# Norm behind the feed-forward part from three sums, half of the modulation moved, and a convolution that opens with two blocks

## The reference, cut to what matters

```python
# end of the first block
h = rmsnorm(x, g_ff_pre)
y = square(relu(h @ w_ff1)) @ w_ff2            # 1024 -> 4096 -> 1024
x = x + rmsnorm(y, g_ff_post)
# start of the second block, layer 0; a second layer (i = 1) follows with the mixer hgrn2
mod = silu(c) @ ada_w[i] + ada_b[i]            # 1024 x 6144 for each of 2 layers
sh1, sc1, g1, sh2, sc2, g2 = split(mod, 6)
h = rms_norm(x, norm1_g[i]) * (1 + sc1) + sh1
a, gate = split(h @ conv_w_in, 2)              # 1024 -> 2 x 1024
u = a * sigmoid(gate)
y = depthwise_conv(u, width 31) + dw_b         # 31 taps for each feature
y = silu(layer_norm(y)) @ conv_w_out
x = x + g1 * y
h = rms_norm(x, norm2_g[i]) * (1 + sc2) + sh2
x = x + g2 * (square(relu(h @ mlp_w1[i])) @ mlp_w2[i])
```

## Time and profile before

| | us |
|---|---|
| median of 3 runs | 2105.71 (2105.07 to 2106.84) |
| profiled execution, own time | 2106.69 |
| its span | 2104.9 |
| TensorE matmul busy | 2058.6 (98%) |
| VectorE busy | 1243.4 (59%) |
| ScalarE busy | 833.4 (40%) |
| POOL busy | 210.9 (10%) |
| mean granted TensorE clock | 0.995 |

### The profile page before, as it was taken

The page is one execution under the profiler, slowest core; times in us unless marked ns, Lnnn a source line. Parts: engine busy times, 40 slices in busy tenths (PEclk is TensorE's granted clock), DMA queues, the critical chain, the costliest instruction groups (busy, mean ns, idle before and its releaser), DMA issues.

```text
span 2104.9 us, 27545 instructions
## 1 busy us (share of the span) xinstructions
PE 2058.6 (98%) x11206; PEld 1668.5 (79%) x11206; DVE 1243.4 (59%) x1951; ACT 833.4 (40%) x1362; POOL 210.9 (10%) x182
## 2 busy tenths in 40 slices
PE   8999999999999999999999999999999989999998
PEld 7787987678878886666988888888887779888887
DVE  5566746446677777986644344476776756343443
ACT  5345544445323233225523233355464544232232
POOL 1321011010000004552000000100000010000002
PEclk9999999999999999999999999999999999999999
DMA  6313422026677762662233332221221232323331
GB/s 203 113 58 100 152 93 88 21 62 219 222 278 256 261 233 92 180 163 84 94 122 100 99 99 83 73 72 51 61 81 51 81 98 83 114 89 97 100 101 40
DMA packets 219710, 245.56 MB, mean 117 GB/s; under 512 B 9272, under 2 KB 205368, under 8 KB 213440
## 3 DMA queue, kind: packets, MB, share of 16 engines
q1 hardware_dynamic: 209360, 231.20, 33.9%
q10 hardware_dynamic: 10224, 12.61, 2.4%
HBM read 237.75 MB, written 3.78 MB: 115 GB/s over the span
## 4 chain that ended last, share of the span: by engine, by line
PE 86%; DVE 6%; ACT 4%; DMA 3%; issue 1%; POOL 0%; ACTq 0%; SPq 0%; DVEq 0%; POOLq 0%
PE bank L1439 24%; PE bank L1443 23%; PE bank L1447 23%; PE bank L1465 2%; PE bank L1473 2%; PE bank L1469 2%; DMA raw<-in_hgrn_in 1%; DVE wL L2067 1%; PE bank L1625 1%; PE bank L1575 1%; PE bank L1533 1%; PE bank L1510 1%; ACT wH L1693 1%; PE bank L1518 1%; PE bank L1558 1%
## 5 line engine op out<-in xcount | busy, mean ns | idle before, releaser
L1439 PE MATMUL bank<-hH,wH 128*128 128x512 f32 (+1 forms) x1768 | 641.8, 385 | 22.4 <-ACT wH L1698 8.0
L1447 PE MATMUL bank<-hL,wH 128*128 128x512 f32 (+1 forms) x1768 | 625.0, 376 | 0.1
L1443 PE MATMUL bank<-hH,wL 128*128 128x512 f32 (+1 forms) x1768 | 624.3, 375 | 0.0
L1693 ACT ACTIVATE wH<-raw 128x1024 fp32r<-128x1024 f32 (+1 forms) x376 | 333.7, 937 | 377.8 <-PE bank L1447 291.1
L2067 DVE TENSOR_TENSOR wL<-raw,wH 128x1024 fp32r<-128x1024 f32 (+1 forms) x340 | 379.3, 1153 | 132.2 <-ACT wH L1693 132.1
L1439 PEld LDWEIGHTS bank<-hH,wH 128*128 128x128 f32 x1768 | 326.7, 189 | 106.5 <-issue 34.3
L1447 PEld LDWEIGHTS bank<-hL,wH 128*128 128x128 f32 x1768 | 327.2, 189 | 61.4 <-DVE hL L2087 0.7
L1443 PEld LDWEIGHTS bank<-hH,wL 128*128 128x128 f32 x1768 | 327.4, 189 | 59.2 <-issue 2.2
L1439 PE MATMUL bank<-hidH,wH 128*128 128x512 f32 (+1 forms) x800 | 305.1, 381 | 1.9 <-ACT hidH L1857 1.9
L1447 PE MATMUL bank<-hidL,wH 128*128 128x512 f32 (+1 forms) x800 | 304.6, 381 | 0.0
L1443 PE MATMUL bank<-hidH,wL 128*128 128x512 f32 (+1 forms) x800 | 304.4, 381 | 0.0
(11 more groups left out here) (224 smaller groups left out, 2020.9 us busy)
## 6 DMA issues: line engine op xcount, KB each, us to landing
raw<-in_mlp SPq DMA_DIRECT2D x64, 1024.0 KB, 5.3
araw<-in_ada_w SPq DMA_DIRECT2D x48, 1024.0 KB, 5.1
raw<-in_w_ff SPq DMA_DIRECT2D x32, 1024.0 KB, 7.4
raw<-in_hgrn_in SPq DMA_DIRECT2D x32, 512.0 KB, 3.8
raw<-in_w_in SPq DMA_DIRECT2D x11, 1024.0 KB, 5.4
raw<-in_conv_in SPq DMA_DIRECT2D x16, 512.0 KB, 3.9
u<-conv_u ACTq DMA_DIRECT2D x24, 270.0 KB, 4.9
raw<-in_w_mv SPq DMA_DIRECT2D x4, 1024.0 KB, 5.4
```

The costliest lines, as they stand in the source:

```text
L1439: mm(out, wH[:, s, m:m + 128], xh[:, k, c], start=k == 0, stop=False)
L1443: mm(out, wL[:, s, m:m + 128], xh[:, k, c], start=False, stop=False)
L1447: i = mm(out, wH[:, s, m:m + 128], xl[:, k, c], start=False, stop=k == KB - 1)
L1693: do(wH[:, s, c], raw[:, r, c], ACT.Copy).then_inc(*s_whi.up(n, x))
```

## The change

- **The seam.** While the last quarter's output blocks come out, VectorE also forms gain times y times x for each block and adds it in `psum`, and ScalarE forms the square of gain times y, which POOL adds in `qsum` (`join_part`). The sum of x squared is kept from the norm ahead of this part (`xsq`). With r the root for y, the mean square of the new x is then that of x, plus 2 r times the cross sum, plus r squared times the square sum. `join` makes it from three products with ones on TensorE and five steps on VectorE, so that the root of the following norm doesn't wait for the new x. The eight squares of the new x and the second `close` go. `post` and `post_x` of block j + 2 stand between `mod` and `mod_lo` of block j. All of `post_x` is on VectorE.
- **The modulation.** Chunks 0 to 2 (layer 0) stay in the first feed-forward part, at 0.35 side steps instead of 0.52 for each step. Chunks 3 to 5 are woven into the second one at the same rate.
- **The opening of the convolution.** `both` takes pieces of 256 columns, which VectorE splits, and covers blocks 0 and 1: four products side by side for k = 0 to 3, then block 0 and block 1 in turn for k = 4 to 7. The order of items up to block 3 is written out anew: TensorE does the projection of block 2 ahead of the taps of block 0. Block 0 has 11 taps on VectorE instead of 15, and five groups of four on TensorE instead of four.

```diff
-BY_POOL = (0, 2, 4, 5)
+BY_POOL = ()
...
-RW, RM = 1.87, 0.52
+RW, RM = 1.87, 0.35
+JOIN_BUSY = 6
+CHUNKS = (0, 1, 2), (3, 4, 5)
...
-    return 15 if blk < KB - 1 else 11
+    return 11 if blk in (0, KB - 1) else 15
...
-        self.lin.put(b, ("act", "ln", tag))
+        self.lin.put(b, ("act", "xsq" if tag == "ff_pre" else "ln", tag))
...
-        if nxt is None:
-            rb, free = self.lin.get()
-            self.close(tag, 1024, busy=BUSY, out=(rb, free))
-            for j in range(KB):
-                pool = j in BY_POOL
-                z, free = (None, ()) if pool else self.lin.get()
-                self.do("post", tag=tag, src=src, j=j, rb=rb, z=z, after=free)
-                self.do("post_x", tag=tag, src=src, j=j, pool=pool, z=z)
-                if not pool:
-                    self.lin.put(z, ("dve", "x", tag, j))
-            for j in range(KB):
-                self.square_mm(tag, j)
-            self.lin.put(rb, ("dve", "post", tag, KB - 1))
...
-    def mod_norm(self, tag, before):
-
-        self.close(tag, 1024, busy=BUSY)
-        run(self.scale(tag, before, None))
+    def join_part(self, j):
+
+        for kind, key in (("cross", ("dve", "cross")), ("gsq", ("act", "gsq"))):
+            s, free = self.tmps.get() if j else (None, ())
+            self.do(kind, j=j, s=s, free=free)
+            if j == KB - 1:
+                self.tails[kind] = s
+            elif j:
+                self.tmps.put(s, ("dve" if kind == "cross" else "pool", kind + "_sum", j))
...
+    def join(self):
+
+        (by, fy), (bq, fq), (bp, fp), (rb, fr), (w, fw) = (*(self.lin.get() for _ in range(4)), self.tmps.get())
+        self.do("join", by=by, bq=bq, bp=bp, rb=rb, w=w, after=(*fy, *fq, *fp), root_free=fr, sum_free=fw, total=self.acc,
...
+        self.lin.put(by, ("act", "ln", "ff_post"))
+        self.lin.put(bq, ("dve", "join", 0))
+        self.lin.put(bp, ("dve", "join", 1))
...
+        b, after = self.lin.get()
+        self.do("busy", tag="join", n=JOIN_BUSY, b=b, after=after)
+        self.lin.put(b, ("mm", "busy", "join"))
...
+        def post(j):
+            if j < KB:
+                self.do("post", tag="ff_post", src="yff", j=j, rb=rb, z=None)
+
+        def add(j):
+            if j < KB:
+                self.do("post_x", tag="ff_post", src="yff", j=j, pool=j in BY_POOL, z=None)
+
+        for j in range(2):
+            post(j)
+            add(j)
+        for j in range(KB):
+            s, free = self.tmps.get()
+            self.do("mod", tag="c1", j=j, s=s, half=None, after=(*free, self.x_event("ff_post", j)))
+            post(j + 2)
+            self.do("mod_lo", tag="c1", j=j, s=s, half=None)
+            self.tmps.put(s, ("lo", "c1", j))
+            add(j + 2)
...
+                    self.join_part(j)
...
-            for ch in range(6):
+            for ch in chunks:
...
-                    if k == 4 and ch:
+                    if k == 4 and ch > chunks[0]:
...
-        run(weave(self.ffn("ff_pre", "w_ff1", 0, "w_ff2", 0, ("h", "ff_pre"), True, to_y), ada(), RM, start=-12.0))
-        self.post_pre("ff_post", None, "yff")
-
-
-        self.mod_norm("c1", "ff_post")
-        do("ada_mod", ch=5)
+            for _ in range(6):
+                yield
+            do("ada_mod", ch=chunks[-1])
+
+        run(weave(self.ffn("ff_pre", "w_ff1", 0, "w_ff2", 0, ("h", "ff_pre"), True, to_y), ada(CHUNKS[0]), RM, start=-12.0))
+        self.join()
...
-            ns = [self.take("conv_in", 0, c, 128, ahead=c == 0) for c in (0, 1024)]
+            ns = [self.take("conv_in", 0, c, 256, ahead=c == 0) for c in (0, 1024)]
             parts = []
-            for n, t in zip(ns, "ag"):
-                b, free = self.lin.get()
-                parts.append(dict(n=n, m=0, b=b, after=free, key=("lin", (t, 0), 0), j=0))
-            for k in range(0, KB, 2):
-                do("lin", nc=128, src=src, width=T, parts=parts, ks=(k, k + 1))
+            for blk in range(2):
+                for n, t in zip(ns, "ag"):
+                    b, free = self.lin.get()
+                    parts.append(dict(n=n, m=128 * blk, b=b, after=free, key=("lin", (t, blk), 0), j=0))
+            for k in range(0, 4, 2):
+                do("lin", nc=256, src=src, width=T, parts=parts, ks=(k, k + 1))
                 if k == 2:
                     self.lows()
+            for blk in range(2):
+                for k in range(4, KB, 2):
+                    do("lin", nc=256, src=src, width=T, parts=parts[2 * blk:2 * blk + 2], ks=(k, k + 1))
             for n in ns:
-                self.piece_done[n] = parts[1]["key"]
-            for p, ev in zip(parts, (to_a, to_u(0))):
-                self.lin.put(p["b"], *ev(p["key"][1], 0, p["b"]))
+                self.piece_done[n] = parts[-1]["key"]
+            for blk in range(2):
+                for p, ev in zip(parts[2 * blk:2 * blk + 2], (to_a, to_u(blk))):
+                    self.lin.put(p["b"], *ev(p["key"][1], 0, p["b"]))
+                copies(blk, frees[blk])
+                if blk == 0:
+                    taps_dve(0, range(6))
             self.highs(ns[1] + NSPLIT)
-            do("shift_first", blk=0, slot=slots[0], after=())
             self.lows()
...
+        def copies(blk, free):
+            if direct(blk):
+                do("shift_first", blk=blk, slot=slots[blk], after=free)
+            else:
+                do("park", blk=blk)
+            do("shift", blk=blk, slot=slots[blk], after=free)
...
-        for blk in range(KB):
+        def diagonal(blk):
+            slots[blk], free = shifts.get()
+            do("wdiag", blk=blk, k0=conv_first(blk), slot=slots[blk], after=free)
+            return free
+
+        frees = [diagonal(blk) for blk in range(2)]
+        both()
+        taps_dve(0, range(6, conv_first(0)))
+        taps_dve(1, range(8))
+        run(self.linear(("a", 2), "conv_in", 0, 256, 128, src, to_a, nc_=128))
+        run(self.linear(("g", 2), "conv_in", 0, 1280, 128, src, to_u(2), nc_=128))
+        b = taps_pe(0)
+        copies(2, diagonal(2))
...
+        taps_dve(1, range(8, conv_first(1)))
+        conv_sum(0, b)
+        taps_dve(2, range(9))
+        run(self.linear(("a", 3), "conv_in", 0, 384, 128, src, to_a, nc_=128))
+        b = taps_pe(1)
+        conv_sum(1, b)
+        taps_dve(2, range(9, conv_first(2)))
+        free = diagonal(3)
+        run(self.linear(("g", 3), "conv_in", 0, 1408, 128, src, to_u(3), nc_=128))
+        copies(3, free)
+        b = taps_pe(2)
+        taps_dve(3, range(5))
+        conv_sum(2, b)
+        taps_dve(3, range(5, conv_first(3)))
+        for blk in range(4, KB):
...
-        run(self.ffn("mlp1", "mlp1", 0, "mlp2", 0, ("h", "m1"), False,
-                     lambda q: self.to_x("m1x", (0, 5), "c1x", q == 3, q), between=m1["second"], norm=r1))
+        run(weave(self.ffn("mlp1", "mlp1", 0, "mlp2", 0, ("h", "m1"), False,
+                     lambda q: self.to_x("m1x", (0, 5), "c1x", q == 3, q), between=m1["second"], norm=r1), ada(CHUNKS[1]), RM, start=-4.0))
...
+        psum, qsum = araw[:, 0, 0:T], araw[:, 0, T:2 * T]
...
-            return name == "conv_in" or name == "conv_out" and c0 < 512
+            return name == "conv_in" and nc_ == 128 or name == "conv_out" and c0 < 512
...
+                elif kind == "join":
+                    by, bq, bp = (banks[it[x]][:] for x in ("by", "bq", "bp"))
+                    for ev in it["total"]:
+                        pe.wait_ge(*event(ev))
+                    mm(by, ones, nacc[:], start=True, stop=False)
+                    pe.wait_ge(*s_dve.at("cross_sum", KB - 2))
+                    mm(bp, ones, psum, start=True, stop=False)
+                    pe.wait_ge(*s_act.at("sq", "ff_post", KB - 1))
+                    mm(by, ones, tmp[:, it["ty"], :], start=False, stop=True).then_inc(*s_mm.up("join", "y"))
+                    pe.wait_ge(*s_pool.at("gsq_sum", KB - 2))
+                    mm(bq, ones, qsum, start=True, stop=False)
+                    pe.wait_ge(*s_act.at("gsq", KB - 1))
+                    mm(bq, ones, tmp[:, it["tq"], :], start=False, stop=True).then_inc(*s_mm.up("join", "q"))
+                    pe.wait_ge(*s_dve.at("cross", KB - 1))
+                    mm(bp, ones, tmp[:, it["tp"], :], start=False, stop=True).then_inc(*s_mm.up("join", "p"))
...
+                    if it["tag"] == "ff_pre":
+                        act.wait_ge(*event(plan.x_event("mem_post", KB - 1)))
+                        do(xsq[:], banks[it["b"]][:], ACT.Copy).then_inc(*s_act.up("xsq", it["tag"]))
...
-                    act.wait_ge(*event(plan.x_event(it["tag"], it["j"])))
-                    do(tmp[:, it["s"], :], xT[:, it["j"], :], ACT.Square).then_inc(*s_act.up("sqm", it["tag"], it["j"]))
...
+                        act.wait_ge(*s_dve.at("ada", CHUNKS[0][-1], KB - 1, 1))
+                    do(tmp[:, it["s"], :] if j else qsum, yff[:, j, :], ACT.Square, scale=vc("ff_post", j)).then_inc(
```

(63 more changed lines are left out.)

126 lines of the change are left out of this document (59 added, 67 removed).

## The result

The changed kernel takes 2111.07 us (median of 9 runs, 2108.66 to 2111.98) against 2105.71 for the kernel before beside it; the ratio is 1.0023, 95% interval [1.0014, 1.0031], so +4.8 by the ratio (+2.9 to +6.5). The forecast was 2108.1 (+2.4) with a range of 2099.5 to 2114. The measured time is within the range, 3.0 above the forecast, and 1.2 above the line of 2109.9 from which "slower" began; the interval lies on both sides of 0.2%.

A forecast was written before the change was run, and what follows sets the result against it. The prediction took TensorE, with 86% of the chain of waits, to bound the kernel. First part -3.9, seam through block 3 +3.3, second part +3.0 gave +2.4 on the median 2105.7: 2108.1 us, range 2099.5 to 2114.

The forecast's parts named there:

- Step 1: First feed-forward part: two column sums at 1.00 fewer and a 1.9 wait gone, extra work hidden; -3.9 us.
- Step 2: Seam between feed-forward part and convolution's projection: sixth sum, its DMA issues and second reduction go; TensorE starts 8.3 earlier.
- Step 3: Two-block opening of the convolution: VectorE's k step 2.83, TensorE waits at k = 5 to 7; only 4.2 left at its end.
- Step 4: Convolution blocks 2 and 3: g2's late split makes TensorE wait 5.1 to 5.4, low clock 1.7; 4.2 becomes a 3.3 loss.
- rival C: Convolution: the low clock costs twice or the park takes 4.5; 2111.2 us; chance 0.14.
- Step 5: Second feed-forward part: three column sums at 1.00, VectorE's added load costs 0; +3.0 us.
- rival B: Second feed-forward part: weight fetches come late behind modulation loads on SyncE's queue; +5.7, 2113.8 us; chance 0.12.
- Rival A: Convolution opening: g2's weights come in time, neither the 5.1 wait nor the 1.7 clock is paid; 2101.3 us; chance 0.24.

The follow-up runs named there:

- e3: Kernel before with only the modulation's chunks 3 to 5 moved to the second feed-forward part, at rate 0.35; 2103.37 us, ratio 0.9985.
- e1: Changed kernel with the split of g2's weights ahead of block 1's park and shift instead of behind them; 2104.02 us, ratio 0.9990.
- e4: Changed kernel with the convolution's two-block opening undone, new seam and moved modulation kept; 2108.88 us, ratio 1.0012.
- e10: Changed kernel with six of the eight adds of y to x on GpSimd instead of VectorE; 2115.95 us, ratio 1.0046.
- e12: Changed kernel with six adds of y to x done on only 8 of 512 columns, computation left out; 2107.73 us, ratio 1.0009.
- e2: Changed kernel with four filling matmuls between a2 and g2, inside the hole; 2108.78 us, ratio 1.0013.
- e9: Changed kernel with g2's split ahead of block 1's copies and the x-square sum in its own bank; 2101.99 us, ratio 0.9980.
- e6: Changed kernel with blocks 0 and 1 side by side for all k steps and ScalarE's items reordered; 2104.21 us, ratio 0.9989.
- e5: Changed kernel with the products of blocks 0 and 1 side by side for all eight k steps; 2112.68 us, ratio 1.0031.
- e7: Changed kernel with the x-square sum ahead of the first feed-forward part in a bank no hidden tile needs; 2108.83 us, ratio 1.0012.
- e8: Changed kernel with all k steps side by side, ScalarE's items reordered and the x-square sum in its own bank; 2100.58 us, ratio 0.9971.

## Why the prediction was right, and where it was off

- **Step 1, the first part, -3.9.** Measured -3.75, but as the sum of two errors, so the hit is luck. Without the copy of the square sum (e3) it is -4.88: two sums at 1.2, not 1.00, and the wait for `hidH`, which between the starts around it (590.89 and 593.14) took 2.0 beyond a matmul and 0.2 just behind. That is 4.6 of the 4.88. The copy, which I called hidden, costs 1.1: the bank of the sum is freed only behind it (`xsq` instead of `ln` in `lin.put`), two ScalarE operations later, and the first hidden tile wants that bank. I priced the copy's 0.6 on ScalarE and did not follow its buffer.
- **Step 2, the seam, TensorE 8.3 earlier.** 8.5. The path of sums, root and VectorE steps came out within 0.2 (maximum 0.43, I had 0.5).
- **Step 3, the opening.** k step 2.81 (forecast 2.83), waits at k = 5 to 7 as written (1.15, 1.14, 0.54; the step of 2.2 came once, ahead of k = 7, where the text has it for k = 6 too, though its 843.1 counts it once), and the size of the end of the opening right: without the hole the ruler is 3.7 shorter than before (e1), forecast 3.5. What I did not draw from this step is that the new norm by itself loses: e4 against e3 shows the sigmoid of block 0 3.9 later, not earlier, with the new norm, because `post` and `add` moved into VectorE's k steps (before, GpSimd made four of the eight adds, and all of them ahead of the projection). I had the number, 2.83 against 1.33, and compared it only with TensorE's 2.72. e10 and e12 show VectorE's pace from both sides; that `post` and `add` are what makes e4 slower than e3 is argued from it and from the waits, since no run has the new norm with them elsewhere on VectorE.
- **Step 4, the hole.** 4.39 + 0.57 = 5.0 (forecast 5.1 to 5.4), and the low clock 1.7 (forecast 1.7). e1 takes both away and gains 7.1, e2 the clock alone and gains 2.3 by the medians, 1.4 by the rows. Steps 2 to 4 together +3.5, forecast +3.3. Between the park's issue at 850.97 and the first issue behind it at 854.66 lie 3.7, against 3.1 in my sum; rival C asked for 4.5 and a second low stretch, and did not happen. The 2.0 that the prediction quotes from the Trainium skill (DMA: Bandwidth & Descriptors, Anatomy of one DMA) is the fixed part of a DMA issued from GpSimd, without its bytes, while the park is issued from ScalarE and moves 271.5 KB; so its estimate of 1.1 less for the wait does not follow, and the measured 3.7 went the other way.
- **Step 5, the second part, +3.0.** Measured +3.7 (and +3.7 in e3): three sums at 1.2, mis-sized because I took the 1.00 of the chain for a sum's price. TensorE's waits in the part are 1.1 and 0.4 before and after, so rival B is out. VectorE took 51 more, where I had 60. No run undid this step alone; its size rests on the rows.
- **Rival A** did not happen in the kernel as changed, and is what e1 makes of it: I gave it 2101.3, and e1 measured 2104.0. e9's 2102.0 is closer only because it has the sum's bank too.

By its steps the forecast of +2.4 came out at +3.5: the wait of g2, its clock and the seam are right, and 0.7 of the rest is the price of a sum. The runs say +4.8 (+2.9 to +6.5), which leaves +2.4 out: the mechanism is right and the size too small. What lies between is the 1.4 ahead of the change, whose place is known and whose cause stays open, and the scatter of single profiles: for e3, too, its profile is 5.4 shorter in span than the one of before, its median 2.8.

## What to carry to other kernels

Starting the wide engine earlier is worth only what the feeding engine's step allows: when work is moved from ahead of a loop into its steps, compare the feeder's step before and after (1.33 and 2.81 here), not the feeder's step with the consumer's. For each instruction added, ask which buffer's release moves behind it; here 0.6 of work on an engine with room cost 1.1. Price a small insertion between matmuls by the starts of its neighbours (1.2 here), not by its own length (1.00). And read an in-order queue as a whole: a weight split standing behind thirteen DMA issues cost 7.1, and moving two lines of the plan got them back.

## What the runs showed of the hardware

- **The low clock does not follow from the idle time alone.** A wait of 2.02 ahead of the first k step left the granted clock at 1.00 in 820 to 824 in the changed kernel and at 0.62 in 822 to 826 in e6. TensorE's records ahead of it are the same in both: six pairs of ones-matmuls and twelve filling ones, without a gap from the feed-forward part on, then idle for 2.02. Of the nine other profiles with this wait (e1, e2, e5, e7 to e12), only e2's is low there (0.62 in 820 to 824). I know no rule from these runs that tells them apart. In e6 and e2 the second k step starts 4.42 behind the first instead of 2.84, so 1.6 later. In e6 1.3 of it is left at k = 7 (33.48 behind the last feed-forward matmul, 32.2 in e5 and e8); in e2 nothing is (31.55, and 31.56 in the changed kernel), since TensorE has waits at k = 5 to 7 that take it up, as the prediction had said.
- **A few filling matmuls keep the clock** through a wait of 5 (e2, with four: 1.00 in all three stretches, 0.88, 0.50 and 0.91 without).
- **GpSimd is no free second VectorE.** Its add of 1.28 stretched a VectorE operation of two SBUF tensors from 0.75 to 1.78, in each of the six steps of e10 in which the two met, so moving 0.69 away cost 0.42 a step. One `mod` of e10 (840.65) took 1.75 instead of 0.74 beside GpSimd's `wdiag`, which had started at 840.34.
